# Gate spread of the PEER layer: up products three tiles ahead, half of the column one-hots on ScalarE, index tables turned ahead of the gates

## The reference, cut to what matters

```python
    v1, i1 = lax.top_k(s1, PEER_TOPK)
    v2, i2 = lax.top_k(s2, PEER_TOPK)
    cand = (v1[..., :, None] + v2[..., None, :]).reshape(B, S, PEER_HEADS, PEER_TOPK * PEER_TOPK)
    cand_idx = (i1[..., :, None] * PEER_NKEYS + i2[..., None, :]).reshape(B, S, PEER_HEADS, PEER_TOPK * PEER_TOPK)
    top_s, pos = lax.top_k(cand, PEER_TOPK)
    expert = jnp.take_along_axis(cand_idx, pos, axis=-1)
    gate = jax.nn.softmax(top_s, axis=-1)
...
        a = jnp.einsum('cd,ced->ce', x_c, u[e_c])
        w = jax.nn.gelu(a.astype(jnp.float32), approximate=False).astype(x_c.dtype) * g_c
        return jnp.einsum('ce,ced->cd', w, v[e_c])
```

## Time and profile before

| | us |
|---|---|
| median of 3 runs | 2765.28 (2764.92 to 2767.57) |
| profiled execution | 2766.01 |
| its span | 2764.2 |
| PE busy | 2687.6 (97%) |
| DVE busy | 1890.7 (68%) |
| ACT busy | 1222.0 (44%) |

### The profile page before, as it was taken

One profiled execution on the slowest core, in us unless ns is written; L12 is line 12 of the kernel. 1 busy time (PEld: TensorE's weight loads), 2 busy tenths in 40 slices (PEclk: granted clock), 3 DMA queues, 4 the chain that ended last, 5 costly groups with the idle time before them and its releaser, 6 DMA issues.

```text
span 2764.2 us, 47464 instructions
## 1 busy us (share of the span) xinstructions
PE 2687.6 (97%) x16264; PEld 2302.3 (83%) x16264; DVE 1890.7 (68%) x3552; ACT 1222.0 (44%) x1999; POOL 158.9 (6%) x126
## 2 busy tenths in 40 slices
PE   6999999989999999999998999999999999999999
PEld 4888888757878888788887799996999999888888
DVE  6877336577777535877338765557699999777765
ACT  5322225455422224322226754467454555454544
POOL 0000003200100001000003010000160000000000
PEclk9999999999999999999999999999999999999999
DMA  7555332211455432555332255652476555777754
GB/s 280 184 186 192 110 100 82 86 62 62 152 188 190 148 107 99 198 183 193 110 100 85 72 165 182 220 175 81 157 228 196 193 197 196 231 238 242 241 196 137
DMA packets 144848, 445.37 MB, mean 161 GB/s; under 512 B 16080, under 2 KB 44880, under 8 KB 144208
## 3 DMA queue, kind: packets, MB, share of 16 engines
q1 hardware_dynamic: 112896, 409.51, 43.8%
q10 hardware_dynamic: 31824, 34.09, 3.6%
HBM read 428.33 MB, written 15.20 MB: 160 GB/s over the span
## 4 chain that ended last, share of the span: by engine, by line
PE 80%; DVE 12%; issue 3%; ACT 2%; DMA 1%; DVEq 1%; SPq 0%; POOL 0%; ACTq 0%
PE bank L2120 21%; PE bank L2121 20%; PE bank L2122 20%; PE bank L2701 13%; DVE spread L1967 3%; DVE w_lo L1261 2%; DVE spread L1963 2%; PE bank L2348 1%; PE bank L2443 1%; DVEq L1967 1%; PE bank L2528 1%; PE bank L2170 1%; DMA ada_start<-w_stream_dram 1%; PE bank L2547 1%; ACT w_hi L695 1%
## 5 line engine op out<-in xcount | busy, mean ns | idle before, releaser
L2120 PE MATMUL bank<-H,w_hi 128*128 128x256 f32 (+1 forms) x3344 | 1102.0, 330 | 8.7 <-DVE w_lo L1261 5.3
L2122 PE MATMUL bank<-H,w_lo 128*128 128x256 f32 (+1 forms) x3344 | 1077.6, 322 | 0.0
L2121 PE MATMUL bank<-H,w_hi 128*128 128x256 f32 (+1 forms) x3344 | 1077.4, 322 | 0.0
L1261 DVE TENSOR_TENSOR w_lo<-raw,w_hi 128x1024 fp32r<-128x1024 f32 x605 | 738.0, 1226 | 395.2 <-ACT w_hi L695 394.5
L695 ACT ACTIVATE w_hi<-raw 128x1024 fp32r<-128x1024 f32 x628 | 660.1, 1052 | 231.8 <-PE bank L2122 192.4
L2120 PEld LDWEIGHTS bank<-H,w_hi 128*128 128x128 f32 x3344 | 636.2, 190 | 81.5 <-issue 21.4
L2121 PEld LDWEIGHTS bank<-H,w_hi 128*128 128x128 f32 x3344 | 636.5, 190 | 51.5 <-issue 4.3
L2122 PEld LDWEIGHTS bank<-H,w_lo 128*128 128x128 f32 x3344 | 636.2, 190 | 49.3
L1416 DVE SCALAR_TENSOR_TENSOR part<-ada_side,cs,part 128x512 f32<-128x512 f32 x420 | 288.3, 745 | 2.3 <-DMA ada_side<-w_stream_dram 2.2
L2120 PE MATMUL bank<-act_hi,w_hi 128*128 128x512 f32 (+1 forms) x770 | 267.4, 347 | 0.0
L2122 PE MATMUL bank<-act_hi,w_lo 128*128 128x512 f32 (+1 forms) x770 | 266.9, 347 | 0.0
(11 more groups left out here) (244 smaller groups left out, 2387.2 us busy)
## 6 DMA issues: line engine op xcount, KB each, us to landing
raw<-w_stream_dram SPq DMA_DIRECT2D x636, 512.0 KB, 3.4
ada_side<-w_stream_dram SPq DMA_DIRECT2D x120, 512.0 KB, 3.9
gelu_scratch<-gelu ACTq DMA_DIRECT2D x108, 128.0 KB, 1.8
gelu_in<-gelu_scratch ACTq DMA_DIRECT2D x108, 128.0 KB, 3.4
ada_start<-w_stream_dram SPq DMA_DIRECT2D x16, 512.0 KB, 14.4
bias<-bias_in_dram ACTq DMA_DIRECT2D x1, 3072.0 KB, 10.0
X<-x_in_dram SPq DMA_DIRECT2D x1, 2048.0 KB, 10.3
mem<-mem_in_dram SPq DMA_DIRECT2D x1, 1024.0 KB, 7.0
```

The costliest lines, as they stand in the source:

```text
L1261: nc.vector.tensor_tensor(w_lo[:, s, :], raw[:, s, :], w_hi[:, s, :].bitcast(F32), ALU.subtract).then_inc(lo_ready, 1)
L2120: nc.tensor.matmul(to, w_hi[:, s, cut], hi, start=first, stop=False, skip_group_check=True)
L2121: nc.tensor.matmul(to, w_hi[:, s, cut], lo, start=False, stop=False, skip_group_check=True)
L2122: return nc.tensor.matmul(to, w_lo[:, s, cut], hi, start=False, stop=last, skip_group_check=True)
```

## The change

It moves, in the gate spread alone:

- Two of the four column matrices of each group go from DVE to ACT (`columns`). [...] DVE keeps columns 0 and 1 and all rows.
- PE starts up tiles 0 and 1 of the stage before the transposes and tile 2 behind them; then it runs spread k, up tile k + 3. From group 20 the lead is 2, from 40 it is 1, from 60 it is 0 (`LEADS`, in iterations of four groups); at groups 20, 40 and 60 no up tile follows. The six products on zeros are gone.
- The four transposes of the indices wait for `peer_chosen` (the last `sel`), and only the two of the gates wait for `peer_routed`. ACT does split and gelu of the stage's first tile ahead of the index copies. DVE makes its columns of group 0 before the gates arrive.

```diff
@@ constants, buffers
+LEADS = (5, 10, SPREAD_GROUPS // R - 1)
+        column_off = sb("column_off", [P, 2, P], peer_at + 11 * KB + 512, F16)
@@ act
+            early(0, 0, at=ROUTE_CHUNKS)
             for n in range(3):
                 act.wait_ge(of("peer", "idx_tr"), n + 1)
                 nc.scalar.activation(idx_T[:, n, :], bank[n][:, 0:NT], ACT.Copy).then_inc(of("peer", "idx_ready"), 1)
+
+            def columns(i, q):
+                k = R * i + q
+                tok = TOKENS_PER_GROUP * k
+                if not (isinstance(k, int) and k < 2):
+                    act.wait_ge(of("peer", "spread"), k - 1)
+                if not (isinstance(k, int) and k < 1):
+                    act.wait_ge(of("peer", "columns"), k)
+                for n in range(2):
+                    ins = nc.scalar.activation(column_off[:, n, :], iota16[:, :], ACT.Abs, scale=-1.0,
+                                               bias=idx_T[:, 1, bass.ds(tok + 2 + n, 1)])
+                ins.then_inc(of("peer", "column_off"), 1)
+                act.wait_ge(of("peer", "column_off"), k + 1)
+                nc.scalar.activation(spread2[:, q % 2, 2:4, :], column_off[:, :, :], ACT.Relu, scale=-1.0, bias=1.0
+                                     ).then_inc(of("peer", "columns"), 1)
+
+            act.wait_ge(of("peer", "idx_ready"), 2)
+            act.wait_ge(of("peer", "iota16_ready"), 1)
+            columns(0, 0)
...
             def spread_step(i, q, first=False):
                 k = R * i + q
-                early(i, q, at=ROUTE_CHUNKS)
                 if not (first and q == 0):
+                    early(i, q, at=ROUTE_CHUNKS)
                     gates_out(k - 1, (q - 1) % R, TOKENS_PER_GROUP * (k - 1))
+                columns(i + (q + 1) // R, (q + 1) % R)
@@ dve
-                    link(ins)
+                    if t == a == 1:
+                        ins.then_inc(of("peer", "chosen"), 1)
+                    else:
+                        link(ins)
...
+            def columns(q, tok):
+                for n in range(2):
+                    nc.vector.tensor_scalar(spread2[:, q % 2, n, :], iota16[:, :], idx_T[:, 1, bass.ds(tok + n, 1)], None,
+                                            ALU.is_equal)
+
+            dve.wait_ge(of("peer", "idx_ready"), 2)
+            columns(0, 0)
...
-                for n in range(TOKENS_PER_GROUP):
-                    nc.vector.tensor_scalar(spread2[:, q % 2, n, :], iota16[:, :], idx_T[:, 1, bass.ds(tok + n, 1)], None,
-                                            ALU.is_equal)
+                if not (first and q == 0):
+                    columns(q, tok)
@@ pe
-            keep_warm(bank[3], 6)
-            pe.wait_ge(of("peer", "routed"), 1)
...
+                pe.wait_ge(of("peer", "columns"), k + 1)
...
+            def up_ahead(i, q, lead):
+                early_up(i + (q + lead) // R, (q + lead) % R, at=ROUTE_CHUNKS)
+
+            early_up(0, 0, at=ROUTE_CHUNKS)
+            early_up(0, 1, at=ROUTE_CHUNKS)
+            pe.wait_ge(of("peer", "chosen"), 1)
...
+            early_up(0, 2, at=ROUTE_CHUNKS)
+            pe.wait_ge(of("peer", "idx_ready"), 3)
             for q in range(R):
-                early_up(0, q, at=ROUTE_CHUNKS)
                 spread(0, q, True)
+                up_ahead(0, q, 3)
+            with pe.Fori(1, LEADS[0]) as i:
+                for q in range(R):
+                    spread(i, q)
+                    up_ahead(i, q, 3)
+            for n, lead in enumerate((2, 1)):
+                for q in range(R):
+                    spread(LEADS[n], q)
+                    if q:
+                        up_ahead(LEADS[n], q, lead)
+                with pe.Fori(LEADS[n] + 1, LEADS[n + 1]) as i:
+                    for q in range(R):
+                        spread(i, q)
+                        up_ahead(i, q, lead)
+            for q in range(R):
+                spread(LEADS[2], q)
+                if q:
+                    up_ahead(LEADS[2], q, 0)
```

More of the change, by code:

```diff
@@ L2651, in _, with spread @@
                     early_up(i, q)
-            keep_warm(bank[3], 6)
-            pe.wait_ge(of("peer", "routed"), 1)
-            for n in range(3):
-                for t in range(2):
-                    src = sel[:, n, t, :] if n < 2 else gate_tok[:, t, :]
-                    ins = nc.tensor.transpose(bank[n][:, t * P:(t + 1) * P], src, ident)
-                ins.then_inc(of("peer", "idx_tr"), 1)
-            def spread(i, q, first):
+            def spread(i, q, first=False):
                 k = R * i + q
                 pe.wait_ge(of("peer", "gated"), k + 1)
-                if first:
-                    pe.wait_ge(of("peer", "idx_ready"), 3)
-                else:
+                pe.wait_ge(of("peer", "columns"), k + 1)
+                if not first:
                     pe.wait_ge(of("peer", "gates"), k - 3)
@@ L2672, in spread @@
                 ins.then_inc(of("peer", "spread"), 1)
+            def up_ahead(i, q, lead):
[3 more added lines that the diff above has]
+            pe.wait_ge(of("peer", "chosen"), 1)
+            for n in range(3):
+                if n == 2:
+                    pe.wait_ge(of("peer", "routed"), 1)
+                for t in range(2):
+                    src = sel[:, n, t, :] if n < 2 else gate_tok[:, t, :]
+                    ins = nc.tensor.transpose(bank[n][:, t * P:(t + 1) * P], src, ident)
+                ins.then_inc(of("peer", "idx_tr"), 1)
+            early_up(0, 2, at=ROUTE_CHUNKS)
+            pe.wait_ge(of("peer", "idx_ready"), 3)
             for q in range(R):
-                early_up(0, q, at=ROUTE_CHUNKS)
                 spread(0, q, True)
-            with pe.Fori(1, SPREAD_GROUPS // R - 1) as i:
+                up_ahead(0, q, 3)
+            with pe.Fori(1, LEADS[0]) as i:
                 for q in range(R):
-                    early_up(i, q, at=ROUTE_CHUNKS)
-                    spread(i, q, False)
-            for q in range(R - 1):
-                early_up(SPREAD_GROUPS // R - 1, q, at=ROUTE_CHUNKS)
-                spread(SPREAD_GROUPS // R - 1, q, False)
-            spread(SPREAD_GROUPS // R - 1, R - 1, False)
-            early_up(SPREAD_GROUPS // R - 1, R - 1, at=ROUTE_CHUNKS)
+                    spread(i, q)
[13 more added lines that the diff above has]
+                    up_ahead(LEADS[2], q, 0)
             pe.wait_ge(of("peer", "ident_kept"), 1)
```

3 lines of the change are left out of this document (2 added, 1 removed).

## The result

The changed kernel takes 2779.39 us (median of 5 runs, 2778.17 to 2783.72), the kernel before 2767.57 (5 runs, 2764.92 to 2767.76): 1.0047 times as long, interval 1.0037 to 1.0058. By the medians it is slower by 12 us, as forecast in direction, where the forecast had 16.

The account below looks back on a forecast made before the run. PE and DVE were taken as even before, ACT as the bound after: 56 steps of 3.60 us, two end turns of 5.91 plus 1.5 each, then 8.4, made +15.9 us. Forecast 2781 us; 8-in-10 range 2767 to 2791.

Parts of the forecast that it names:

- What bounds the kernel before: Gate spread: PE and DVE need about the same time per group, 3.38 and 3.37 us; ACT has only 0.84 free.
- The columns: Two columns per group on ACT: two Abs, a wait and a Relu cost 1.06 us, bounds 0.88 to 1.31.
- ACT's step: In the spread's loops ACT needs 2.54 + 1.06 = 3.60 us a group against PE's 3.38, setting the pace.
- the cheaper rival: ACT's step in the loops is only 3.43 to 3.50 us, giving 2771 to 2776 us; chance 0.10.
- Which engine waits where: Within each spread group PE stands about 0.22 us, waiting for ACT, and DVE is idle about 0.5.
- Head start: Stage start: PE gains two up tiles, 5.8 us less 0.2, worth something only if PE sets the pace.
- A gap at group 41: PE's gate spread: a gap of 0.7 us, counted only in the rival where PE keeps the pace.
- The turns: Steps 61 and 62, lead zero: PE and ACT alternate, 5.91 us a turn against 3.38, plus 1.5 for half clock.
- Sum: Gate spread to second down tile: reached at 2368.8 instead of 2352.87, +15.9 us, so a median of 2781.
- PE keeps the pace: Rival: ACT's step is 3.38 us or less, turns eat the head start; 2765.9, or 2768.9 with the clock; chance 0.17.
- the head start is kept: Rival: PE keeps the pace and the end turns do not hold it; -8 us, about 2758; chance 0.05.

Follow-up runs that it names:

- e9: The changed kernel with PE's order of before: only the two columns on ACT, no leads, no early transposes; 2774.02 us, 1.0026 of the kernel before.
- e2: The changed kernel with one of four columns on ACT instead of two, DVE making three; 2771.15 us, 1.0016 of the kernel before.
- e1: The changed kernel with the next group's columns made before gelu and G in ACT's last three steps; 2774.22 us, 1.0037 of the kernel before.
- e7: The changed kernel with the Relu of ACT's columns made twice; 2809.35 us, 1.0152 of the kernel before.
- e4: The changed kernel without ACT's columns: DVE makes all four, PE keeps its leads and earlier transposes; 2771.33 us, 1.0019 of the kernel before.
- e10: e8 with ACT issuing the four loads of the first gelu tiles before its last three groups; 2763.56 us, 0.9987 of the kernel before.
- e3: The changed kernel with the edits of e1 and e2 together; 2768.12 us, 1.0004 of the kernel before.
- e8: e3 with DVE making one-hots ahead of the low part in the last four groups; 2766.25 us, 0.9993 of the kernel before.
- e12: e10 with the leads of the up tiles run down later; 2762.34 us, 0.9989 of the kernel before.

## Why the prediction was right

- *What bounds the kernel before*: right. DVE and PE are even, and ACT's 0.84 us free (0.90 by the 1.01 below) are less than the columns take. e9 (two columns, PE's order of before) is slower by 7.3 us, e2 with one column keeps 3.38 as far as group 44.
- *The columns*: 1.06 forecast, 1.03 measured. The two Abs are 0.39 each (0.68 together) and the Relu 0.42, as read from rows 8; the 1.03 that came of the Trainium skill's prices ("ScalarE: Activation LUTs", section "What ACT_TABLE_LOAD costs") is the measured number. The advice of that page of the Trainium skill ("Rules for kernel authors") against relu and the like on ScalarE held as well: the two columns took 0.33 on DVE and take 1.03 on ACT.
- *ACT's step*: 3.60 forecast, 3.51 measured. The mis-sized terms are gelu to G, 1.01 where I took 1.07, and the columns by 0.03; over 56 steps the two are 5 us. Why gelu to G is shorter now stays open: before, the gelu was 0.39 long and G began 0.20 behind the issue of the store, now it is 0.36 and 0.14, and in both groups shown the spread had ended, 0.66 and 0.51 us before G. By its size the step sits at the edge between my forecast (3.50 to 3.72) and the cheaper rival.
- *Which engine waits where*: DVE waits 0.4 in each group (0.5 forecast). PE's 0.13 a group (0.22 forecast, as a gap) does not show as a gap of the products, whose ends are modelled. The weight loads are busy 190 us of the 200 where it was 197, but 3 of these 7 us are the gap at group 41. That PE stands is shown by the spreads, 14.0 us for four where they were 13.52.
- *Head start*: as forecast (spread 0 is 10.15 behind tile 43, forecast 10.2) and worthless, since PE is not the bound here.
- *A gap at group 41* of 2.80 I had only in a rival. The up tile behind it ran at half clock, and one ACT step became 4.90: 1.4 us. e1, which is the same kernel there, has the same gap (2.81) at full clock and no such step.
- *The turns*: right in place and mechanism. Two gaps of 2.57 and 2.56 (2.5 forecast), 7.58 and 7.61 us for a turn where 5.91 + 1.5 = 7.41 was forecast. The 1.5 for the clock was read from one row, and it came out partly by luck: other runs have gaps of this length without half clock (last section).
- *Sum*: with the 4.1 us late start taken off, ACT's step 4 begins at 2140.85 (2140.7 forecast), step 60 at 2338.7 (2342.3), the second down product at 2366.5 (2368.8). So +13.6 where I had +15.9: -5.2 for the step, +1.4 for group 41, +1.3 behind step 60, and +0.2 from the start. The profiled time 2783.7 is the forecast's 2781.9 with the 4.1 us that were lost ahead of the stage and less the 2.3 by which the stage was over-priced. The median came within 2 us of the forecast's 2781 because before's median, over five runs, was 2.3 higher than the 2765.3 that I started from; the change itself is 12 us by the medians and 13 by the ratio.
- *The rivals*: "PE keeps the pace" falls with e7; "the head start is kept" falls with e4, where it was paid back though ACT had no columns. e4 also shows what the prediction did not see: the leads cost by themselves (2 us in the trace, 5 by the ratio), where DVE cannot follow and through its queue at the end.

What stays open: why ACT stands 0.27 at its loop edges with one column. And what makes up the 4 us of the profiled execution ahead of the stage. In 1990 to 2112 one group of DVE operations was slower, here before and after:

```profile
L1891 DVE TENSOR_TENSOR cand<-top_v 128x256 f32<-128x256 f32 x16 | 5.7, 416 | 0.0
```

```profile
L1916 DVE TENSOR_TENSOR cand<-top_v 128x256 f32<-128x256 f32 x16 | 7.9, 552 | 0.0
```

This is 2.2 us of the 4, and it is not the change's. In all 14 traces the group takes either 5.7 or 7.9 us, seven each. The seven with 5.7, e1 with the whole change among them, end tile 43 at 2121.2 or before, and the seven with 7.9 at 2121.7 or behind. What makes it slow, and the rest of the 4 us, no run isolates.

## What to carry to other kernels

Before work goes to an engine with a low busy share, write down one period of it by starts, with the DMA issues and the waits for its own results: here 57% busy was 75% taken, and the step grew past the period. A head start for one engine is worth only what the others can follow (nothing in e4, most of two up tiles in e10); where it is taken back, look which queue holds the next operand behind something that it doesn't need. At an end, mend all links at once: e1, e3 and e8 each left a gap or moved the wait to the next link, and only with the last link mended too (e10, e12) was the time below the kernel before by its interval, by 0.1%.

## What I had not expected of the hardware

The length of a gap does not say whether half clock follows. Two pairs of runs have the same instructions on PE around a gap of the same length: after and e1 at spread 41 (2.80 and 2.81 us), e2 and e3 at spread 61 (2.76 both). The first 3 us of the up tile behind it, in this order (the clock is the third number from the end):

```profile
2275.90:2278.90 3.00, 3.00 (x20) 3.00 (x18) 3.00 (x7) 2.33 (x6) 0.00 (x0) 0.57 0.50 167
2271.20:2274.20 3.00, 3.00 (x28) 2.89 (x24) 2.98 (x7) 2.33 (x6) 0.00 (x0) 1.00 0.47 145
2332.30:2335.30 3.00, 3.00 (x29) 2.95 (x26) 2.77 (x8) 0.00 (x0) 0.00 (x0) 1.00 0.52 169
2337.60:2340.60 3.00, 3.00 (x17) 3.00 (x16) 2.40 (x8) 0.00 (x0) 0.00 (x0) 0.50 0.56 183
```

The whole tile took 4.45 us in after and 5.27 in e3, and about 3.0 in e1 and e2. Of the gaps before a spread, the shortest that half clock followed is 2.16 us (e2, spread 63), and none of 2.06 or less was followed by it. But those of 2.17 and 2.76 in e2, 2.18 in e12, 2.53 (spread 41) and 2.56 (spread 63) in e4, 2.67 in e9 and 2.81 in e1 were not either. What decides it no run here shows, so a price of 1.5 us for a single gap of this length is a guess. And ACT's columns under a register-addressed bias took what the line between the rows with a fixed one gave: 0.39.
